# Sample tokens as four partition strips in the output and down projections, and a regrouped end of the FFN

## The reference, cut to what matters

```
x  = x + (gate_conv * conv_out + gate_attn * attn_out) @ w_out     # w_out: 2048 x 2048
hf = rms_norm(x, g_ffn)
x  = x + (silu(hf @ w_gate) * (hf @ w_up)) @ w_down                # hidden width 5632
y  = rms_norm(x, g_final)                                          # prompt and sample tokens
```

## Time and profile before

| what | value |
|---|---|
| median of 3 runs | 2281.44 us (2281.4 to 2434.7) |
| the profiled execution | 2280.5 us, span of its slowest core 2279.0 us |
| PE busy | 2125.6 us, 93% of the span |
| DVE / ACT busy | 755.2 us (33%) / 435.3 us (19%) |
| spans of the 8 cores | 2271.9 to 2279.0 us |
| granted TensorE clock, mean | 0.974 to 0.978 |

### The profile page before, as it was taken

The page is one execution under the profiler, slowest core; times in us unless marked ns, Lnnn a source line. Parts: engine busy times, 40 slices in busy tenths (PEclk is TensorE's granted clock), DMA queues, the critical chain, the costliest instruction groups (busy, mean ns, idle before and its releaser), DMA issues.

```text
span 2279.0 us, 35092 instructions; the slowest of 8 cores (2271.9 to 2279.0 us)
## 1 busy us (share of the span) xinstructions
PE 2125.6 (93%) x13817; PEld 1301.8 (57%) x13817; DVE 755.2 (33%) x1163; ACT 435.3 (19%) x778; POOL 67.3 (3%) x118
## 2 busy tenths in 40 slices
PE   1699997999999999999799999999999999999985
PEld 1455554665554666666578656556556556556541
DVE  2433435222322322222134141441441432432435
ACT  3533334332223311111022100000000000000022
POOL 0000000000000000000000000000000000000000
PEclk9799999999999999999899999999999999999996
DMA  8253132439768797776822827527535435434203
GB/s 232 75 107 83 39 70 61 104 82 156 133 124 134 129 163 133 132 131 112 200 62 36 151 56 129 97 53 131 98 67 102 84 56 101 71 70 76 50 26 129
DMA packets 42157, 230.34 MB, mean 101 GB/s; under 512 B 4603, under 2 KB 16507, under 8 KB 26851
## 3 DMA queue, kind: packets, MB, share of 16 engines
q0 software_dynamic: 27552, 137.37, 36.1%
q1 hardware_dynamic: 14443, 90.72, 14.8%
HBM read 349.72 MB, written 59.99 MB: 180 GB/s over the span
## 4 chain that ended last, share of the span: by engine, by line
PE 88%; DMA 4%; ACT 3%; DVE 3%; issue 2%; SPq 0%; DVEq 0%; ACTq 0%; POOLq 0%
PE ps L125 88%; DMA arena<-xext 3%; DVE arena L125 3%; ACT arena L125 3%; DMA arena<-wout 1%; DMA arena<-state 0%; SPq L142 0%; ACT L125 0%; DVEq L85 0%; ACTq L85 0%; SPq L85 0%; POOLq L85 0%
## 5 line engine op out<-in xcount | busy, mean ns | idle before, releaser
L125 PE MATMUL ps<-arena 128*128 128x347 bf16 (+8 forms) x13817 | 2125.6, 318 | 138.6 <-DVE arena L125 112.5
L125 PEld LDWEIGHTS ps<-arena 128*128 128x128 bf16 (+2 forms) x13817 | 1301.8, 101 | 961.9 <-issue 188.5
L125 DVE TENSOR_TENSOR arena<-ps,arena 128x512 f32<-128x512 f32 (+7 forms) x791 | 459.4, 583 | 943.1 <-PE ps L125 715.9
L125 ACT ACTIVATE arena<-ps 128x347 f32<-128x347 f32 (+2 forms) x285 | 133.9, 479 | 1129.7 <-PE ps L125 1128.3
L125 ACT ACTIVATE arena<-arena 128x1 f32<-128x1 f32 (+6 forms) x139 | 114.8, 830 | 181.0 <-DVE arena L125 157.5
L125 DVE SCALAR_TENSOR_TENSOR arena<-ps,arena 128x347 f32<-128x347 f32 (+3 forms) x75 | 43.4, 579 | 276.4 <-PE ps L125 263.5
L125 DVE TENSOR_TENSOR arena<-arena 128x1040 f32<-128x1040 f32 (+7 forms) x167 | 122.8, 742 | 35.7 <-ACT arena L125 22.1
L125 ACT COPY arena<-ps 128x512 bf16<-128x512 bf16 (+7 forms) x155 | 93.6, 619 | 160.9 <-PE ps L125 159.2
L125 DVE SCALAR_TENSOR_TENSOR arena<-arena 128x2048 bf16<-128x2048 f32 (+3 forms) x35 | 82.3, 2351 | 79.6 <-ACT arena L125 79.6
L125 ACT CAST arena<-ps 128x384 bf16<-128x384 f32 x72 | 37.0, 514 | 178.3 <-PE ps L125 176.7
L125 ACT ACTIVATE arena<-ps,arena 128x357 f32<-128x357 f32 (+3 forms) x40 | 21.2, 530 | 137.6 <-PE ps L125 136.4
(11 more groups left out here) (12 smaller groups left out, 22.1 us busy)
## 6 DMA issues: line engine op xcount, KB each, us to landing
arena<-wgu POOLq DMA_DIRECT2D x44, 1024.0 KB, 8.2
arena<-wgate POOLq DMA_DIRECT2D x16, 1408.0 KB, 17.7
arena<-w_down POOLq DMA_DIRECT2D x11, 2048.0 KB, 18.0
arena<-wqkv POOLq DMA_DIRECT2D x9, 2048.0 KB, 21.2
arena<-xext SPq DMA_DIRECT2D x16, 1024.0 KB
kso<-ck SPq DMA_DIRECT2D x16, 1022.0 KB
vso<-cv SPq DMA_DIRECT2D x16, 1022.0 KB
arena<-wglu POOLq DMA_DIRECT2D x8, 1024.0 KB, 9.9
```

Source lines behind the costliest of these rows:

```text
L125: self.q[eng].append(lambda e, meth=meth, a=a, kw=kw, s=s: getattr(e, meth)(*a, **kw).then_inc(s, 1))
```

## The change

Five things are altered.

1. **Sample tokens in strips.** The 16 sample tokens are no longer a ninth tile. Their 2048 output columns are cut into eight blocks of 256, block `j + 4h` lying in partitions 32j to 32j+31 and columns 256h to 256h+255 of one 128 x 512 buffer `xS`. `wout_sample` and `down_sample` issue matmuls with a stationary operand of 32 columns (16 of them zeros) to the four partition strips of one accumulator in turn. The norm's sum over the strips is a small matmul with the constant `fold`.
2. **Output projection** in two passes of four chunks each, chunks 0 to 3 and then, tile by tile, chunks 4 to 7. Three of the eight tiles of residual are loaded whole during the gates, and of the other five columns 0 to 255; after the gate loop come five pieces of 768 columns, then five of 1024.
3. **Copies.** In the last six gate steps none is issued; the FFN issues three instead of two after each block.
4. **First gate_up** split: its pieces 0 and 1 stand ahead of the transposes of tile 7, piece 2 behind.
5. **End.** `down(9)` is no longer issued after `gate_up(40)`. Blocks 9 and 10 are accumulated together, 8 matmuls to a group; the last block of `w_down` goes to the place of two `gate_up` slots. The scaling of tile t-1 stands behind the second addition of tile t, and for tile 7 squares and scaling are cut in pieces.

The core of the diff:

```
+        XACC = [R0, R0 + 2048, R0 + 8256, R0 + 4096, R0 + 6144, HTO, HTO + 2048, HTO + 4096]
...
+        S.op('pool', lambda e: e.memset(xS, 0.0), [], ['xS'])
+        S.op('pool', lambda e: e.memset(mixS[:, :, :], 0.0), [], ['mixS'])
+        for t in range(3):
+            S.dma('sp', xacc[t], xext[1024 + 128 * t:1152 + 128 * t, :], writes=[XK[t], XK[t] + 'r'])
+        S.dma('sp', xst, xext[1408:2048, 0:256].rearrange("(t p) c -> p t c", p=128), writes=['xst'])
+        for j in range(4):
+            for h in range(2):
+                S.dma('sp', xS[32 * j:32 * j + 16, 256 * h:256 * h + 256], xs_d[:, 1024 * h + 256 * j:1024 * h + 256 * j + 256], writes=['xS'])
+
+        def gS_load(row):
+            for j in range(4):
+                for h in range(2):
+                    S.dma('sp', gS[32 * j:32 * j + 32, 256 * h:256 * h + 256], gb_d[row:row + 1, 1024 * h + 256 * j:1024 * h + 256 * j + 256].partition_broadcast(32), writes=['gS'])
+
+        gS_load(1)
...
-        S.dma('sp', xst[:, 0:4, :], xext[1024:1536, 0:256].rearrange("(t p) c -> p t c", p=128), writes=['xst'])
-        S.dma('sp', xst[0:16, 4, :], xs_d[:, 0:256], writes=['xst'])
-        S.dma('sp', xst2[:, :, :], xext[1536:2048, 0:256].rearrange("(t p) c -> p t c", p=128), writes=['xst2'])
...
-            copy_piece(1)
+            if n < 10:
+                copy_piece(1)
...
-        ORDER = [8] + list(range(8))
-        S.dma('sp', xacc[8][0:16, 256:2048], xs_d[:, 256:2048], writes=[XK[8] + 'r'])
-        for t in range(8):
-            S.dma('sp', xacc[t][:, 256:2048], xext[1024 + 128 * t:1152 + 128 * t, 256:2048], writes=[XK[t] + 'r'])
+        for (a_, b_, x) in ((256, 1024, 'rA'), (1024, 2048, 'rB')):
+            for t in range(3, 8):
+                S.dma('sp', xacc[t][:, a_:b_], xext[1024 + 128 * t:1152 + 128 * t, a_:b_], writes=[XK[t] + x])
...
-        for c in range(2):
+        S.op('dve', lambda e: e.tensor_copy(out=mixS[:, :, 0:16], in_=mixT[:, :, 1024:1040]), ['mixT8'], ['mixS'])
+
+        def wout_sample(cs):
+            for k in range(KC):
+                for c in cs:
+                    ws, wkey = wo_w(c)
+                    j, h = c % 4, c // 4
+                    S.op('pe', lambda e: e.matmul(PS[6][32 * j:32 * j + 32, 256 * h:256 * h + 256], lhsT=mixS[:, k, :], rhs=ws[:, k, :], start=(k == 0), stop=(k == KC - 1), skip_group_check=True),
+                         ['mixS', wkey], [PSK[6]])
+
+        for c in range(4):
             ws, wkey = wo_w(c)
-            for t in ORDER:
+            for t in range(8):
...
-            wo_load(6 + c)
+                    xi, xik = xo, XK[t] + 'rA'
+                S.op('dve', lambda e: e.tensor_tensor(out=xo, in0=PS[bk][:, 0:256], in1=xi, op=ALU.add), [PSK[bk], xik], [XK[t]])
+            if c == 0:
+                wout_sample((0, 1))
+                wo_load(6)
+            if c == 1:
+                wo_load(7)
+            if c == 3:
+                wout_sample((2, 3))
...
-        for idx, t in enumerate(ORDER):
-            np_ = TNP[t]
-            for cp in range(3):
+        def sample_rstd():
+            S.op('act', lambda e: e.activation(out=sqS, in_=xS, func=AF.Square, accum_out=ssqS), ['xS'], ['hS', 'ssqS'])
+            S.op('pe', lambda e: e.matmul(PS[7][:, 0:1], lhsT=fold, rhs=ssqS, start=True, stop=True), ['fold', 'ssqS'], [PSK[7]])
+            S.op('act', lambda e: e.activation(out=rsS, in_=PS[7][:, 0:1], func=AF.Ln, scale=1.0 / D, bias=eps_norm), [PSK[7], 'epsc'], ['rsS'])
+            S.op('act', lambda e: e.activation(out=rsS, in_=rsS, func=AF.Exp, scale=-0.5), ['rsS'], ['rsS'])
+
+        S.alias(['hS'], ['xst'])
+        for t in range(8):
+            for cp in range(2):
...
+            if t == 0:
+                wout_sample((4, 5, 6, 7))
+                S.op('dve', lambda e: e.tensor_tensor(out=xS, in0=PS[6][:, :], in1=xS, op=ALU.add), [PSK[6], 'xS'], ['xS'])
+            if t == 2:
+                sample_rstd()
+                S.op('dve', lambda e: e.scalar_tensor_tensor(out=hS, in0=xS, scalar=rsS, in1=gS, op0=ALU.mult, op1=ALU.mult), ['xS', 'rsS', 'gS'], ['hS'])
...
+        def down_sample(hss):
+            bk = 4 + (dctr[0] % 4)
+            dctr[0] += 1
+            for hi, hs in enumerate(hss):
+                a_q, w, wk = aq[hs % 2], wds[hs == NHS - 1], 'wdL' if hs == NHS - 1 else 'wd'
+                for k in range(4):
+                    for j in range(4):
+                        S.op('pe', lambda e: e.matmul(v3(PS[bk][32 * j:32 * j + 32, :], 2), lhsT=a_q[:, k, 1024:1056], rhs=mkap(w[:, k, 256 * j:256 * j + 1], [[1024, 2], [1, 256]]),
+                                                      start=(hi == 0 and k == 0), stop=(hi == len(hss) - 1 and k == 3), skip_group_check=True),
+                             ['aq%d' % (hs % 2), wk], [PSK[bk]])
+            S.op('dve', lambda e: e.tensor_tensor(out=xS, in0=PS[bk][:, :], in1=xS, op=ALU.add), [PSK[bk], 'xS'], ['xS'])
...
+        def down_mm(t, j, hss):
+            bk = 4 + (dctr[0] % 4)
+            dctr[0] += 1
+            for hi, hs in enumerate(hss):
+                a_q, w, wk = aq[hs % 2], wds[hs == NHS - 1], 'wdL' if hs == NHS - 1 else 'wd'
+                for k in range(4):
+                    S.op('pe', lambda e: e.matmul(PS[bk][:, :], lhsT=a_q[:, k, 128 * t:128 * t + 128], rhs=w[:, k, 512 * j:512 * (j + 1)], start=(hi == 0 and k == 0), stop=(hi == len(hss) - 1 and k == 3)),
+                         ['aq%d' % (hs % 2), wk], [PSK[bk]])
+            xo = xacc[t][:, 512 * j:512 * (j + 1)]
+            S.op('dve', lambda e: e.tensor_tensor(out=xo, in0=PS[bk][:, :], in1=xo, op=ALU.add), [PSK[bk], XK[t]], [XK[t]])
...
+                n = 4 * hs + n4
+                if n == 0:
+                    gate_up(0, (0, 1))
+                    a5_T(7)
+                    gate_up(0, (2,))
+                else:
+                    gate_up(n)
+                if n4 == 0 and 1 <= hs < NHS - 1:
                     down(hs - 1)
-                    copy_piece(2)
-        down(NHS - 1)
+                    copy_piece(3)
+                if hs == NHS - 1 and n4 == 1:
+                    S.alias(['wdL'], ['gu1', 'gu2'])
+                    wd_load(NHS - 1)
         copy_piece(len(copies))
...
+        down_sample(LAST2)
+        for t in range(8):
+            for j in range(4):
+                down_mm(t, j, LAST2)
+                if t == 7:
+                    S.op('act', lambda e: e.activation(out=hb5[1][:, 512 * j:512 * j + 512], in_=xacc[7][:, 512 * j:512 * j + 512], func=AF.Square, accum_out=ssq4[:, j:j + 1]), [XK[7]], ['hb51', 'ssq4'])
+                if j == 1 and t >= 1:
+                    final_scale(t - 1, 0, 2048)
+                if j == 1 and t == 0:
+                    sample_rstd()
+                if j == 3 and t == 0:
+                    S.op('dve', lambda e: e.scalar_tensor_tensor(out=xS, in0=xS, scalar=rsS, in1=gS, op0=ALU.mult, op1=ALU.mult), ['xS', 'rsS', 'gS'], ['xS'])
+                    for jj in range(4):
+                        for h in range(2):
+                            S.dma('sp', ys_d[:, 1024 * h + 256 * jj:1024 * h + 256 * jj + 256], xS[32 * jj:32 * jj + 16, 256 * h:256 * h + 256], reads=['xS'], writes=['ys%d%d' % (jj, h)])
+            if t < 7:
+                final_stats(t)
+                final_rstd(t)
+        S.op('dve', lambda e: e.tensor_reduce(out=ssq[1], in_=ssq4, axis=AX.X, op=ALU.add), ['ssq4'], ['ssq1'])
+        final_rstd(7)
+        final_scale(7, 0, 1024)
+        final_scale(7, 1024, 2048)
```

More of the change, by code:

```diff
@@ L246, in build_program @@
     hv_d = din("hv", [128, 1])
+    fold_d = din("fold", [128, 128])
     y_d = dout("y", [1024, D])
@@ L624, in build_program @@
         p0_keys = ['hb', 'hb_b', 'ubb0', 'ubb1', 'ucb0', 'ucb1', 'sg', 'u2', 'stT', 'cps0', 'cps1', 'css0', 'css1']
[L625 removed]
+        first = ['tabA', 'tabB', 'tabC', 'qb0', 'qb1', 'kb', 'ra', 'rb', 'peS'] + ['qT%d' % b for b in range(8)]
         early = first + ['cT%d' % n for n in range(8)]
[L627 removed]
+        late1 = ['vb0', 'vb1', 'vb2', 'kT0', 'kT1', 'kT2', 'numS', 'denS', 'pS', 'pSn']
         late2 = ['pT0', 'pT1', 'stS', 'sbS', 'qkS0', 'qkS1', 'qkS2', 'vnS0', 'vnS1', 'vnS2']
@@ new lines, in build_program @@
+        o = R0 + 10304
+        xS = af(o, 512); o += 512
+        gS = af(o, 512); o += 512
+        fold = af(o, 128); o += 128
+        mixS = v3(ab(o, 256), 16); o += 256
+        assert o <= ARENA_WORDS
+        hS = ab(YR + 6976, 256)
+        early_x = ['xacc0', 'xacc1', 'xacc2', 'xS', 'gS', 'fold', 'mixS']
+        S.alias(early_x + [k + 'r' for k in early_x], first + late)
+        S.op('pool', lambda e: e.memset(xS, 0.0), [], ['xS'])
+        S.op('pool', lambda e: e.memset(mixS[:, :, :], 0.0), [], ['mixS'])
@@ L1253, in build_program, with gate_up @@
         wd_load(0)
-        a5_T(ORDER[-1])
         S.dma('sp', gbc, gb_d[2:3, :].partition_broadcast(128), writes=['gbc'])
```

(24 more changed lines are left out.)

124 lines of the change are left out of this document (67 added, 57 removed).

## The result

The changed kernel takes 2170.95 us, the median of 4 runs (2170.49 to 2171.76). The ratio to the kernel before is 0.9516, 95% interval 0.9493 to 0.9539. The forecast was 2168 us, in a range of 2156 to 2192.

What follows compares the result with a forecast made beforehand. PE was taken as the bound, busy 2125.6 of 2279.0 us, so only fewer columns or pauses help. Savings of 42.2 + 53.5 + 17.4 = 113.1 us gave 2165.9, plus 2.4 for the median: 2168 us, range 2156 to 2192.

Steps and rivals of the forecast that it cites:

- stretches A and B: End of gates to end of first gate_up, then to end of gate_up(43): 42.2 and 53.5 us saved.
- stretch C: From the end of gate_up(43) to the end of the span: 85.1 us becomes 67.7, saving 17.4.
- Strips: Sample matmuls in four partition strips overlap: 1.1 us per down instead of 3.55, 8.4 in the output projection instead of 14.7.
- Drain at the change of width: At 13 places the skill's rule charges an engine drain when tiling mode changes; the forecast added nothing for it.
- The residual: Output projection: five 384 KB pieces at 109 KB per us land about 1107 to 1110, wanted at 1117; no wait.
- The rival of slow short rows: Residual loads share by rows, 47 KB per us, last piece 13 us late: say 2181 us; chance 0.08.
- Norm of tile 7 under two pieces of `gate_up`: First gate_up: the 6.1 us norm runs under pieces 0 and 1 (9.4 us), where PE paused 5.96 us.
- The new wait behind the transposes: First gate_up: piece 2 waits for tile 7 to be copied out of the accumulator, 1.1 us.
- Is C bound by PE?: At the end PE needs 6.95 us a tile, the loop through ScalarE 6.9, so PE sets the pace, barely.
- The tail: Behind the last matmul: addition, square, reduce, tiny activations, two half scalings and a half store, 8.9 us in all.
- The rival on the other side: After the gates TensorE without pauses is granted a lower clock: slower than before, 2430 or about 2410 us; chance 0.03.
- The signs: From 1087: PE idle under 4 us, clock 1.00, gate_up(0) ending about 1230, strips 0.9 to 1.2 us, last chain about 9.

Runs made afterwards that it cites:

- `whole_tiles`: Changed kernel with the residual of tiles 3 to 7 loaded after the gates in five pieces of 1792 columns instead of ten: 2181.1 us (one run).
- `whole_late_copies`: Changed kernel with loads as before: all eight residual tiles in 1792-column pieces after the gates, one copy piece per gate step: 2201.68 us, ratio 0.9655.
- `all_late`: Changed kernel with columns 256 to 2047 of tiles 0 to 2 also loaded after the gates, in 768- then 1024-column pieces: 2171.8 us (one run).
- `unsplit`: Changed kernel with the first gate_up in one piece behind the transposes of tile 7: 2178.40 us, ratio 0.9535.
- `split_keys`: Changed kernel with the last tile's dependences kept per 512 columns instead of for the whole tile: 2166.58 us, ratio 0.9483.

## Where the prediction was right and which step of it failed, point by point

The forecast was 2168, the median 2170.95: 113.1 us were to be saved in the span, and 110.4 were. What was to be saved, and how, came out as forecast in stretches A and B. The step that failed is the last term of stretch C, the work behind TensorE's last matmul: 8.9 us forecast, 14.0 measured. The stretches of the sum:

| stretch | before | forecast | measured | by |
|---|---|---|---|---|
| A, gates to the end of `gate_up(0)` | 185.2 | 143.0 | 141.2 | 1228.67 - 1087.49 |
| B, to the end of `gate_up(43)` | 921.7 | 868.2 | 867.3 | 2095.94 - 1228.67 |
| C, the end | 85.1 | 67.7 | 72.7 | 2168.6 - 2095.94 |

(TensorE's end of a stretch is 0.2 us before the product's start, as in the prediction. The gates end at 1087.49, 0.6 us before the first request for a `w_out` chunk at 1088.09, as they did in before.)

- **Strips: right in kind, too dear in size.** The forecast took 1.1 us for a `down` and 8.4 for the output projection, because it read 0.0656 us as the time that one narrow weight load needs. Measured are 0.97 and 5.6, near the lower bounds (0.89 and 5.2). The reading was wrong: the recorded time of a load isn't what it takes. With four strips a load shows 0.55 / 16 = 0.034 us, with one strip 0.195, for the same load. That was 2.8 us too much in A, and 9 x 0.13 = 1.2 in B.
- **Drain at the change of width.** None is seen: loads of full width resume 0.42 us late behind one, two or four strips in turn, and 0.43 behind the plain sample tile.
- **The residual.** In time for all pieces, as forecast: no addition in A waits for `xext`. The rate of 109 KB per us itself isn't confirmed: where tiles of 896 KB do come late, they land 9.24 us apart in `whole_tiles` and 8.8 and 9.1 in `whole_late_copies`, 97 to 102 KB per us. The rival of slow short rows fell in `all_late`, which brings 60% more of them and still doesn't wait: 8 x 384 KB between their first request at 1088.4 and the addition at 1118.9 are at least 100 KB per us, not 47. Whole tiles would have cost 10 us.
- **Norm of tile 7 under two pieces of `gate_up`.** Right; `unsplit` prices it at 6.4 us. The new wait behind the transposes was put at 1.1 us and is 1.77, because VectorE's half of the copy starts only at 1222.96, when ScalarE's (1221.78, 1.01 us) has ended: both write the one name `mixT7`.
- **Is C bound by PE?** The call "barely" is what the runs show: TensorE 6.90 us a tile, the loop 6.70. TensorE's own end, 2095.94 + 2.2 + 55.6 + 1.0 = 2154.7, is 2154.6 in the trace.
- **The tail: the step that failed.** The forecast put 8.9 us behind the last matmul; there are 14.0. It priced each piece of work and took for granted that pieces of one tile depend only on their own columns. In this program they share a name. The last addition starts 2.1 us later than its matmuls allow, and the second scaling 2.8 us later than the first ends. Of the 2.1, the bracket shows 1.04; the rest comes from further up: tile 7's second addition, at 2152.37, waits for the first square in the same way (its read-out ends at 2152.20) and starts 2.3 us ahead of TensorE's end, where it starts 3.3 ahead in `split_keys`, and it holds up all that follows on VectorE. `split_keys` removes both waits, and 9.1 us are left behind the last matmul: the pieces were priced right, to 0.2 us, and the waits between them were put at nothing. Half cuts were costed as a gain, and their wait was in the kernel to be read: `y_out` reads the name that the next `final_scale` writes.
- **The clock.** The rival on the other side fell: 870 us of B at 1.00, with hardly a pause since the gates. The 13/16 (0.81) of the Trainium skill, TensorE: Matmul & The Clock Gate, section "Seeing it yourself", is in none of these traces.
- **The signs.** PE idles 2.7 us from 1087 us to its last matmul (under 4 forecast), strips take 0.97 us, the two `gate_up` end where they should within 2.1 us, and the tile's pace is 6.90. The one sign that failed is the last tile's chain, about 9 us forecast.

The misses were 1.8 and 0.9 us too long, and 5.0 too short, so they nearly cancelled. That the total is closer than its parts is luck.

## What to carry to other kernels

Work for a few rows costs TensorE as much as for 128 (16 matmuls of 512 columns take 3.56 us for the sample tokens and 6.90 / 2 = 3.45 for half a full tile). Cut its columns into four blocks, send them to the four partition strips of one accumulator, and it costs little more than a quarter (here 0.97 us). When a stage waits for a load, look at the order of its bytes before their number: the same bytes, cut by the pass that needs them, cost nothing where whole tiles cost 10 us. Where a tile's work is cut in pieces, give the pieces names of their own, or the cut buys waits (4.9 us here).
